# Decoder kernel on one core: sample attention of the second layer, scores in four column groups and the value product turned round

## What is computed

```
s = jnp.einsum('bqhjd,bkhjd->bhjqk', q, k) * (DIFF_HEAD_DIM ** -0.5)
s = jnp.where(mask[None, None, None], s, NEG_INF)
p = jax.nn.softmax(s, axis=-1)
a = p[:, :, 0] - lam * p[:, :, 1]
return jnp.einsum('bhqk,bkhe->bqhe', a.astype(v.dtype), v)
```

## Time and profile before

| | |
|---|---|
| median of 3 runs | 1352.97 us (1349.73 to 1354.64) |
| span of the profiled execution | 1347.5 us |
| TensorE busy | 1283.3 us, 95% |
| VectorE, ScalarE, GpSimd busy | 589.0, 405.2, 355.9 us |
| mean granted TensorE clock | 0.960 of full speed |

### The profile page before, as it was taken

The page is one execution under the profiler, slowest core; times in us unless marked ns, Lnnn a source line. Parts: engine busy times, 40 slices in busy tenths (PEclk is TensorE's granted clock), DMA queues, the critical chain, the costliest instruction groups (busy, mean ns, idle before and its releaser), DMA issues.

```text
span 1347.5 us, 23629 instructions
## 1 busy us (share of the span) xinstructions
PE 1283.3 (95%) x9728; PEld 1230.3 (91%) x9728; DVE 589.0 (44%) x867; ACT 405.2 (30%) x746; POOL 355.9 (26%) x290
## 2 busy tenths in 40 slices
PE   6999899999999999999999899889999999999995
PEld 6888899999999999998899677689999999999994
DVE  7656554233333333454435853645433333333334
ACT  6524343212222212333312442533321222221221
POOL 3353023304205105220062200002430420511523
PEclk9989999999999999998899887869999999999997
DMA  7611422222222222223144542302222222222211
GB/s 267 230 50 58 146 93 79 94 81 92 93 79 91 83 90 79 92 94 107 52 128 113 194 141 94 110 17 87 86 94 82 91 94 79 93 81 91 80 60 66
DMA packets 37033, 132.59 MB, mean 98 GB/s; under 512 B 4226, under 2 KB 5122, under 8 KB 36322
## 3 DMA queue, kind: packets, MB, share of 16 engines
q1 hardware_dynamic: 35858, 123.42, 27.6%
q0 software_dynamic: 1104, 8.15, 2.1%
HBM read 121.18 MB, written 7.03 MB: 95 GB/s over the span
## 4 chain that ended last, share of the span: by engine, by line
PE 89%; DVE 7%; ACT 2%; issue 1%; DMA 0%; DVEq 0%; POOL 0%; SPq 0%; ACTq 0%
PE psum L418 77%; PE psum L566 2%; PE psum L550 1%; PE psum L467 1%; PE psum L492 1%; DVE inv_rms L991 1%; DVE weights_split L972 1%; PE psum L555 1%; PE psum L483 1%; ACT weights_split L722 1%; DVE tiny L1079 1%; PE psum L537 1%; PE psum L517 1%; PE psum L495 0%; PE psum L511 0%
## 5 line engine op out<-in xcount | busy, mean ns | idle before, releaser
L418 PE MATMUL psum<-operand_b,weights_split 128*128 128x272 f32 x4416 | 564.1, 290 | 4.0 <-DVE weights_split L972 3.8
L418 PEld LDWEIGHTS psum<-operand_b,weights_split 128*128 128x128 f32 x4416 | 558.9, 190 | 7.0 <-DVE weights_split L972 4.4
L418 PE MATMUL psum<-operand_a,weights_split 128*128 128x272 f32 (+1 forms) x4116 | 533.9, 292 | 24.0 <-DVE weights_split L972 19.0
L418 PEld LDWEIGHTS psum<-operand_a,weights_split 128*128 128x128 f32 x4116 | 528.1, 193 | 28.1 <-issue 20.8
L722 ACT ACTIVATE weights_split<-weights_raw 128x1024 fp32r<-128x1024 f32 (+1 forms) x186 | 192.6, 1036 | 432.3 <-PE psum L418 432.3
L972 DVE TENSOR_TENSOR weights_split<-weights_raw,weights_split 128x1024 fp32r<-128x1024 f32 (+1 forms) x186 | 238.9, 1285 | 136.2 <-ACT weights_split L722 136.1
L1356 POOL TENSOR_TENSOR squares<-staging 128x544 f32<-128x544 f32 x64 | 76.3, 1193 | 471.3 <-ACT operand_a L768 207.6
L1026 DVE TENSOR_TENSOR residual<-psum,residual 128x544 f32<-128x544 f32 x48 | 34.8, 725 | 175.9 <-PE psum L418 175.9
L1007 DVE SCALAR_TENSOR_TENSOR staging<-psum,inv_rms 128x544 f32<-128x544 f32 x56 | 40.6, 725 | 150.1 <-PE psum L418 150.1
L1349 POOL TENSOR_TENSOR squares_sum<-squares_sum,squares 128x544 f32<-128x544 f32 (+1 forms) x35 | 48.5, 1387 | 115.7 <-ACT squares L734 115.2
L1358 POOL TENSOR_TENSOR operand_a<-squares,operand_a 128x544 fp32r<-128x544 f32 x32 | 65.0, 2031 | 2.5
(11 more groups left out here) (195 smaller groups left out, 831.5 us busy)
## 6 DMA issues: line engine op xcount, KB each, us to landing
weights_raw<-in_weights SPq DMA_DIRECT2D x180, 512.0 KB, 3.3
cache_tiles<-in_page_k SPq DMA_DIRECT2D x16, 384.0 KB, 3.9
cache_tiles<-in_page_v SPq DMA_DIRECT2D x16, 384.0 KB, 3.8
cache_tiles<-in_mem_k SPq DMA_DIRECT2D x8, 512.0 KB, 4.9
cache_tiles<-in_mem_v SPq DMA_DIRECT2D x8, 512.0 KB, 5.3
residual<-in_x SPq DMA_DIRECT2D x1, 2176.0 KB, 11.9
out_y<-projected SPq DMA_DIRECT2D x8, 272.0 KB, 2.1
rotated<-projected POOLq DMA_DIRECT2D x4, 408.0 KB, 7.1
```

The costliest lines, as they stand in the source:

```text
L418: mm = pe.matmul(ps[:, 2 * (j % PS) + hf, 0:n], w(wr), act[:, ar, k, hf * n:(hf + 1) * n], start=(q == 0 and wr == 0 and ar == 0), stop=(q ...
```

## The change

The scores of a decode item are written as products of 32 weight columns instead of 64: heads 0 to 3 (g = 0) and heads 4 and 5 (g = 1) of each request go to a row group of 32 of their own, and the four groups (request o, g) take turns. The value product swaps its operands: 32 columns of `pt` are the weights and 384 columns of values (three heads) move, so that each group of 32 PSUM rows holds one request and one half of the heads. Its result has the queries in the rows and must be turned back. ScalarE copies it to the free part of the staging slot (`decode_rows`), TensorE turns it with three transposes into bank 7 (`decode_turn`), and VectorE drains it from there with six copies as before. Two semaphores are new, and `mixed` of a decode item is now raised by `decode_turn`.

```
+        def decode_rows(n):
+            return T[:, n % 2, 4 * GROUP:4 * GROUP + 3 * P]
...
                     for o in range(2):
-                        c = chunk_of(n) + o
-                        chunk_ready(pe, k_loaded, c)
-                        keys = kv[:, c % 2, 0, :].rearrange("p (g h k) -> p h g k", g=PAGES, h=HEADS)
-                        for h in range(HEADS):
-                            pe.matmul(sc[64 * o:64 * o + 64, 0, 0:PAST].rearrange("p (g k) -> p g k", g=PAGES),
-                                      Qbd[:, h, 2 * a + o, :], keys[:, h, :, :], start=(h == 0), stop=(h == 5))
+                        chunk_ready(pe, k_loaded, chunk_of(n) + o)
+                    for r in range(4):
+                        for o, g in ((0, 0), (1, 0), (0, 1), (1, 1)):
+                            h, row = r + 4 * g, 64 * o + 32 * g
+                            if h < HEADS:
+                                keys = kv[:, (chunk_of(n) + o) % 2, 0, :].rearrange("p (g h k) -> p h g k", g=PAGES, h=HEADS)
+                                pe.matmul(sc[row:row + 32, 0, 0:PAST].rearrange("p (g k) -> p g k", g=PAGES),
+                                          Qbd[:, h, 2 * a + o, 32 * g:32 * g + 32], keys[:, h, :, :],
+                                          start=(r == 0), stop=(h in (3, 5)))
...
-                    for h in range(HEADS):
+                    for o in range(2):
+                        chunk_ready(pe, v_loaded, chunk_of(n) + o)
+                    for kt in range(2):
                         for o in range(2):
-                            ...
-                                mm = pe.matmul(ps[:, m0, out:out + GROUP],
-                                               kv[:, c % 2, 1, kt * 768 + h * P:kt * 768 + (h + 1) * P],
-                                               pt[:, GROUP * (2 * kt + o):GROUP * (2 * kt + o + 1)],
+                            for part in range(2):
+                                row, at = 64 * o + 32 * part, kt * 768 + part * 3 * P
+                                mm = pe.matmul(ps[row:row + 32, m0, 0:3 * P],
+                                               pt[:, GROUP * (2 * kt + o):GROUP * (2 * kt + o) + 32],
+                                               kv[:, (chunk_of(n) + o) % 2, 1, at:at + 3 * P],
                                                start=(kt == 0), stop=(kt == 1))
+                    mm.then_inc(decode_mixed, 1)
+                    return
...
+            def decode_turn(n):
+                pe.wait_ge(decode_copied, DECODE.index(n) + 1)
+                for hh in range(3):
+                    mm = pe.transpose(ps[:, 7, lo_of(hh)], decode_rows(n)[:, lo_of(hh)], ident)
                 mm.then_inc(mixed, 1)
...  TensorE's attention(n0, n1)
                     if n + 2 < n1:
                         scores(n + 2)
+                    if n - 2 in DECODE:
+                        decode_turn(n - 2)
                     turn(n)
                     if n > n0:
                         mix(n - 1)
...  ScalarE's attention(n0, n1)
                         items_exp(n + 1)
+                    if n - 2 in DECODE:
+                        act.wait_ge(decode_mixed, DECODE.index(n - 2) + 1)
+                        act.activation(decode_rows(n - 2), ps[:, 7, 0:3 * P], ACT.Copy).then_inc(decode_copied, 1)
                     if n < n1:
                         items_copy(n)
...  VectorE's items_drain(n)
-                        src = ps[:, 7, 2 * GROUP * h:2 * GROUP * (h + 1)].rearrange("p (o c) -> p o c", o=2)[:, :, 4 * h:4 * h + 4]
+                        at = 32 * (h // 3) + 4 * h
+                        src = ps[:, 7, lo_of(h % 3)].rearrange("p (o c) -> p o c", o=2)[:, :, at:at + 4]
```

More of the change, by code:

```diff
@@ L235, in build @@
         new_mixed, new_added = sem("new_mixed"), sem("new_added")
+        decode_mixed, decode_copied = sem("decode_mixed"), sem("decode_copied")
         sub_mean = sem("sub_mean")
@@ L309, in build @@
         DEC = [n for n, it in enumerate(ITEMS) if it[0] in ("memdec", "decode")]
+        DECODE = [n for n, it in enumerate(ITEMS) if it[0] == "decode"]
+        def decode_rows(n):
+            return T[:, n % 2, 4 * GROUP:4 * GROUP + 3 * P]
         block = ctx.enter_context(nc.Block())
@@ L557, in mix @@
                 else:
-                    for h in range(HEADS):
+                    for o in range(2):
+                        chunk_ready(pe, v_loaded, chunk_of(n) + o)
+                    for kt in range(2):
                         for o in range(2):
[L561 to L565, removed]
-                                mm = pe.matmul(ps[:, m0, out:out + GROUP],
-                                               kv[:, c % 2, 1, kt * 768 + h * P:kt * 768 + (h + 1) * P],
-                                               pt[:, GROUP * (2 * kt + o):GROUP * (2 * kt + o + 1)],
-                                               start=(kt == 0), stop=(kt == 1))
+                            for part in range(2):
[3 more added lines that the diff above has]
+                                               kv[:, (chunk_of(n) + o) % 2, 1, at:at + 3 * P],
+                                               start=(kt == 0), stop=(kt == 1))
+                    mm.then_inc(decode_mixed, 1)
+                    return
+                mm.then_inc(mixed, 1)
+            def decode_turn(n):
+                pe.wait_ge(decode_copied, DECODE.index(n) + 1)
+                for hh in range(3):
+                    mm = pe.transpose(ps[:, 7, lo_of(hh)], decode_rows(n)[:, lo_of(hh)], ident)
                 mm.then_inc(mixed, 1)
```

## The result

The changed kernel takes **1318.35 us** (median of 4 runs, 1317.09 to 1320.83), against 1351.82 us for the kernel before (median of 4, 1349.73 to 1354.64). The ratio is **0.9757, with a 95% interval of 0.9729 to 0.9784**: 33.5 us faster. I forecast 1328 with a range of 1319 to 1340.

What follows compares the result with a forecast made beforehand. TensorE was taken to set the pace of the attention stretch, with VectorE's 71 us as floor. Scores 10.7 us plus value product 14.7 gave 25.4 off 1352.97: 1327.6, say 1328 us, range 1319 to 1340.

Steps and rivals of the forecast that it cites:

- Column groups side by side, each at its own pace: Scores and value product on TensorE: four groups of 32 columns run at once, each at the pace of one alone.
- Rival 3: The column groups queue instead of running side by side: 7 us slower, 1360 us; chance 0.03.
- Decode 0's block: From decode 0's value product to the next item's `mix`: 11.52 us before, 5.6 after, net gain 3.2 beside the scores.
- Decode 1's block: From decode 1's value product to the next item's `mix`: 12.08 us before, 5.55 after, net gain 6.5.
- Low clock kept: Assumption in decode 1's walk that TensorE stays at the 1.2 GHz level, so its value product takes 2.57 us.
- Decode 2's block: From decode 2's value product to the next `mix`: 6.39 us before, 3.9 after, net 2.5, with ScalarE's copy on the path.
- Decode 3's: From decode 3's value product to the next `mix`: 9.40 us before, 6.5 after, taken as 2.5 gained; ScalarE's table load delays it.
- The waits: VectorE's wait for decode items' scores on TensorE falls from 18.6 us to about 8; the attention stretch lasts about 100 us.
- rival 4: VectorE and ScalarE take back half of the value product's 14.7 us: 1335 us; chance 0.18.
- rival 2: TensorE's clock is low for longer, since its dense blocks become short: gain only 11 us, 1342 us; chance 0.13.
- Waits costed at nothing: Decode 1's key pages land in time by under 1 us, and value pages are used only three to five items later.
- rival 1: The clock stays high where it was low, 801 to 822 us: gain 30 us, 1323 us; chance 0.17.

Runs made afterwards that it cites:

- e4: The changed kernel with the same score and value products issued group by group instead of the groups taking turns; 1321.7 us.
- e5: The changed kernel, but ScalarE copies the value product before the exponential of the item ahead; 1321.8 us.
- e6: The changed kernel with decode 3 at place 21 of the list instead of 23, so its copy comes before the square root; 1321.9 us.
- e9: The changed kernel, where TensorE fills nine of its waits ahead of transposes with products of 256 columns that nobody reads; 1313.3 us.
- e1: The kernel before with the new page scores alone; value product, its order and its drain stay old; 1334.6 us.
- e3: The kernel before, each value product instruction moving 128 columns instead of 40, so sample values are not computed; 1341.3 us.

## Why the prediction was nearly right and its size was not

- **Column groups side by side, each at its own pace**: right. 1.85 us where 1.82 was forecast, four times, and 1.32 for the value product at full clock where 1.29 was. The rule of the Trainium skill, "TensorE: Matmul & The Clock Gate", Part 3, that was quoted against it (loads overlap running matmuls only in other row groups) does not hold here, and e4 shows that not even the turns are needed for groups of four instructions. Rival 3 is out.
- **Decode 0's block**: 5.75 us (784.03 to 789.78) where 5.6 was forecast.
- **Decode 1's block**: this term was mis-sized. The forecast has "Low clock kept", 5.55 us. It took 4.11 (798.13 to 802.24), the product 2.00 of it instead of 2.57 since the full clock came back during it, and the `mix` and scores behind it ran at full clock. Decode 2's scores, 2.8 in the sum, took 1.85. From the `mix` behind decode 1 to decode 2's product it was 17.82 us and is 13.12: 4.7 gained where the sum had 2.6, since the diff item's products there were priced at the low clock too.
- **Decode 2's block**: 4.03 (815.36 to 819.39), forecast 3.9. **Decode 3's**: 6.39 (833.40 to 839.79), forecast 6.5, and ScalarE's table loads stood in it as said. But e5 and e6 show that ScalarE was not the cause alone: VectorE's chain ends as late. Both blocks came out by some luck: decode 2's product itself ran partly at the low clock, 1.99 us busy, hidden behind ScalarE's exponential.
- **The tail**: the forecast left the low clock from 863 on untouched. Between the last decode item's next `mix` and the projection's first product it had 22.85 us (868.64, to 891.49, where the trace of before has it) and now has 20.29 (839.79 to 860.08): 2.6 us that no term held.
- **The whole walk**: the sum gave a span of 1322.1 us and it was 1315.2, 6.9 less. Besides the terms above, 1.2 us were gained between decode 0's block and decode 1's product and 0.9 behind 891 us, and 1.5 lost before decode 0's scores, all put at nothing. Another 2.4 us of the miss are no work at all: the 5.5 us carried from span to median were partly the spread of single executions, and the distance is 3.2 us for the changed kernel.
- **The waits**: VectorE's wait for L505 was forecast at about 8 us and is 3.6; the stretch of 100 us is 93. VectorE and ScalarE took nothing noticeable back, so rival 4 is out, and rival 2 as well, since the low time fell.
- **Waits costed at nothing** (key pages, value pages): right. In decode 1's scores no gap precedes L501 at 785.35.
- **Chances**: the case that came true is rival 1, "the clock stays high where it was low", given 0.17 and 1323 us. It came true in its condition; its price was still 5 us short, in part because it left out the end of the stretch. The step that failed is that the walk froze the clock as it stood ("Low clock kept", and nothing for the low stretch behind decode 3), where the runs showed 26 to 27 us less at the low level, worth some 10 us. The row of 801 to 822 already showed what mattered: TensorE busy for 20.77 of 21 us and yet at half clock, and the largest thing in it was the very product that the change removes. I read it as a reason against the gap rule and did not ask what in it was sparse. With full-clock prices alone the sum is 10.8 for the scores and 3.2 + 3.2 + 2.5 + 2.5 for the blocks, 22.2 us, and the rest fell by 22; the low time should have been a term of its own. Its size could not have been worked out from the rows on record.

The Trainium skill, "TensorE: Matmul & The Clock Gate", "HAM oscillation", blames gaps for the low clock. For what is left of the low time the runs agree (e9: gaps filled, 23 us less). For the middle stretch they point to another cause (e1, e3): no gap, but a product that moves 40 columns where 128 would pass in the same time. For the end of the stretch, 31 us low before and 14 after, the cause stays open.

## What to carry to other kernels

When a small product moves few columns behind full weight loads, swap its operands: the long side moves, the short side is the weight in a group of 32 columns, and four groups run side by side; turning the result back cost 1 us an item here, and the product fell from 5.4 us to 1.3. Count the time at the low clock as a term of the sum, with its own price from executions that differ in it, and ask of every low stretch which instructions stand in it; a busy engine is no proof that the clock will come up. When TensorE waits are short and another engine is the bound, filling them can pay by the clock alone (5 to 7 us here, the kernels not run side by side).

## What the runs showed of the hardware

- A TensorE that was busy all the time with 48 instructions of 40 moving columns stayed at 1.2 GHz for 10 us (the kernel before and e1); with 128 columns and the same number of weight columns to load it was given 2.4 GHz back 2 us into the product (e3, decode 2).
- The clock fell from 2.4 to 1.2 GHz inside such a product of 40 columns at 862.8 us in the kernel before and at 832.0 us in e1, after more than 6 us without a gap on TensorE. Two other products of the kind, in the kernel before, ran at 2.4 GHz throughout.
- Products in different groups of 32 columns overlap fully with all 128 rows in use and all four writing one PSUM bank: 24 instructions of 256 columns in 1.85 us, about the time of the eight in the longest group (1.72).
- Issued group by group, eight instructions of a group hold back the next group's (2.78 us instead of 1.85), four do not (1.31 us against 1.32).
- Of two executions of the same kernel, the one with 28 us more at the low clock was 10.9 us slower.
